# One inference step of a two-layer decoder: sample states, mixing blocks and the samples' last rows laid out anew

## The reference

```python
# layer 0, branch B: gated linear recurrence; for a sample one step from its stored state
inter = jnp.einsum('bthk,bhkv->bthv', qc * jnp.exp(cb), s)          # 8 samples, 4 heads, 128x128 states
...
# layer 1: causal mean pooling, four channel groups with trailing windows 2, 4, 8, 16
def pool_mixer(h, prev, pos0, w_groups, scale):
    ext = jnp.concatenate([prev, h], axis=1)                         # prev: the last 15 rows (zeros for the prompt)
    for gi, w in enumerate(POOL_WINDOWS):
        win_sum = csum[15 + 1 + t] - csum[15 + 1 + t - w]
        mixed = win_sum / min(w, pos + 1) - h[:, :, group gi]        # mean minus token
        outs.append(einsum('btc,cd->btd', mixed, w_groups[gi]))      # 256 x 256 per group
    return concatenate(outs, -1) * scale
# every layer
x = x + mix
x = x + hier_moe(rmsnorm(x), ...)    # top 1 of 4 groups, top 2 of its 8 SwiGLU experts, 32 experts in all
# at the end
y = rmsnorm(x, norm_final)           # for the prompt and for the samples
```

## Time and profile before

| what | us |
|---|---|
| median of 3 runs | 1458.81 (1457.67 to 1462.44) |
| profiled execution | 1456.91 |
| its span, first to last instruction | 1455.1 |
| PE busy in the span | 1254.0 (86%) |
| DVE busy | 357.2 (25%) |
| ACT busy | 256.1 (18%) |
| DMA, mean over the span | 339 GB/s |

### The profile page before, as it was taken

How to read it: one execution, slowest core, us unless ns; L and a number is a source line. 1 busy time by engine, 2 the same in 40 slices (tenths; PEclk the granted TensorE clock), 3 DMA queues, 4 the chain that set the end, 5 groups by cost and what they waited for, 6 DMA issues and landing times.

```text
span 1455.1 us, 14771 instructions
## 1 busy us (share of the span) xinstructions
PE 1254.0 (86%) x5968; PEld 614.9 (42%) x5968; DVE 357.2 (25%) x824; ACT 256.1 (18%) x440; POOL 83.7 (6%) x101
## 2 busy tenths in 40 slices
PE   7999999999999866878777798999978878888786
PEld 3688865544643322223222235863422222232222
DVE  2056477532431000010100007451010000010006
ACT  3243643333300000000000002520000000000002
POOL 1000000000000100000000000000000000000000
PEclk9999999999999999999999999899999998899998
DMA  9435657427489999999999999389999999999995
GB/s 347 107 71 183 219 162 220 115 88 318 172 349 428 425 401 422 428 427 425 426 427 427 425 413 367 142 305 420 427 428 426 426 430 426 426 427 425 427 415 209
DMA packets 82447, 492.95 MB, mean 339 GB/s; under 512 B 17197, under 2 KB 21965, under 8 KB 59350
## 3 DMA queue, kind: packets, MB, share of 16 engines
q1 hardware_dynamic: 65968, 449.35, 75.9%
q0 software_dynamic: 13568, 37.03, 7.6%
q10 hardware_dynamic: 2862, 5.91, 1.2%
HBM read 479.75 MB, written 36.56 MB: 355 GB/s over the span
## 4 chain that ended last, share of the span: by engine, by line
PE 50%; DMA 39%; DVE 7%; ACT 2%; issue 2%; SPq 0%; ACTq 0%; DVEq 0%
DMA ring<-in_moe_w 37%; PE ps L2241 21%; PE ps L1915 5%; PE ps L1908 4%; PE ps L2167 3%; PE ps L2279 2%; PE ps L2255 1%; PE ps L2226 1%; PE ps L2353 1%; PE ps L2307 1%; PE ps L2266 1%; DVE arena L1371 1%; PE ps L1957 1%; DMA arena<-i_rows 1%; PE ps L2296 1%
## 5 line engine op out<-in xcount | busy, mean ns | idle before, releaser
L2241 PE MATMUL ps<-ring,arena 128*64 128x512 f32 x1920 | 463.5, 640 | 118.5 <-DMA ring<-in_moe_w 117.4
L2241 PEld LDWEIGHTS ps<-ring,arena 128*64 128x64 f32 x1920 | 145.2, 147 | 432.4 <-issue 272.8
L1784 DVE TENSOR_TENSOR arena<-arena,ps 128x512 f32<-128x512 f32 x32 | 22.0, 688 | 775.3 <-ACT arena L1207 775.3
L2279 PE MATMUL ps<-ring,arena 128*64 128x512 f32 x832 | 186.0, 599 | 26.6 <-issue 14.1
L2279 PEld LDWEIGHTS ps<-ring,arena 128*64 128x64 f32 x832 | 68.8, 138 | 127.1 <-issue 112.7
L1207 ACT ACTIVATE arena<-ps 128x512 f32<-128x512 f32 x32 | 19.1, 597 | 584.1 <-PE ps L2241 584.1
L1908 PE MATMUL ps<-arena,ring 128*128 128x260 f32 x512 | 116.9, 387 | 0.9 <-ACT arena L942 0.9
L1908 PEld LDWEIGHTS ps<-arena,ring 128*128 128x128 f32 x512 | 97.0, 193 | 17.3 <-issue 1.7
L1215 ACT ACTIVATE arena<-ps,arena 128x1024 f32<-128x1024 f32 x32 | 35.6, 1114 | 321.2 <-PE ps L2279 276.5
L1915 PE MATMUL ps<-ring,arena 128*128 128x512 f32 x192 | 86.8, 599 | 0.0
L851 POOL DMA_INDIRECT arena<-hn_rows,arena x30 | 30.7, 1022 | 519.6 <-PE ps L2433 474.2
(11 more groups left out here) (312 smaller groups left out, 1053.9 us busy)
## 6 DMA issues: line engine op xcount, KB each, us to landing
ring<-in_moe_w SPq DMA_DIRECT2D x78, 4096.0 KB, 23.3
ring<-in_moe_w SPq DMA_DIRECT2D x40, 1024.0 KB, 12.5
arena<-in_moe_w SPq DMA_DIRECT2D x12, 2048.0 KB, 17.8
ring<-in_w_in SPq DMA_DIRECT2D x6, 2048.0 KB, 20.3
y_rows<-c_zero POOLq DMA_DIRECT2D x2, 4160.0 KB, 18.0
ring<-in_moe_w SPq DMA_DIRECT2D x4, 2048.0 KB, 20.3
ring<-y_rows SPq DMA_DIRECT2D x8, 1024.0 KB, 18.3
arena<-in_x_prompt SPq DMA_DIRECT2D x8, 512.0 KB, 6.2
```

The costliest lines, as they stand in the source:

```text
L2241: last = T.matmul(ps[r_, 2 + j, :], xgT[:, k, r_], w[:, k, :], start=(k == 0), stop=(k == KC - 1))
L2279: last = T.matmul(ps[r_, 5 + c, :], hactT[:, k, r_], w[:, k, c * 512:(c + 1) * 512], start=(k == 0), stop=(k == FC - 1))
```

## The change

**Sample states.** The masked queries become the weights: `qmask` holds for each head and sample 32 columns, of which one is the query and the others zero. The state is the moving operand (128 columns), the four heads write to the four groups of 32 partitions, and the 8 samples add up in PSUM. The result has a row per head and sample; DVE copies it, PE transposes it, and `sample_heads` comes one unit later, `sample_means` too.

**Mixing.** The matrix of the windows has 144 columns, 128 for the block and 16 for what the block carries into the next. One product per chunk does both. Eight chunks of 144 columns don't fit two banks of 512, so they come in three parts; the third reuses the first bank after ACT's copy. The copies lie in two buffers in turn. DVE adds the carry of the block before (`carry_added`), and the maps wait for it.

**Samples.** Their mixture is PE's 8 transposes of the normed rows, scaled and added to `mix_before` by DVE (`samples_mixed`). Maps and last rows put the four quarters of the channels in four column groups, and DVE adds them in four sums (`from_groups`).

**Tail.** PE adds the second row sets of tiles 0, 2 and 3 too, and for the samples both sets and x itself. The order is 0, 1, 2, NT, 3 on PE and SP; DVE's order is written out. The samples' normed rows come straight from PSUM: ACT squares, PE sums over the column groups with `fold`, ACT takes the root, DVE scales; four stores take them out. Five small loads for it are issued by POOL in layer 1's fourth pair.

```diff
@@ sample states, PE
-                        T.matmul(ps[:, 5, h * NB + b:h * NB + b + 1], stv[:, b, h, :], qf[:, h, b:b + 1], start=True, stop=True)
+                        T.matmul(ps[32 * h:32 * h + 32, 5, P:2 * P], qmask[:, h, 32 * b:32 * b + 32], stv[:, b, h, :],
+                                 start=(b == 0), stop=(b == NB - 1), skip_group_check=True, tile_position=(0, 32 * h))
...
+            def turn_sample_rows():                       # after project(SAMPLE0 + 2, 0)
+                pe.wait_ge(snorm_ready, 1)
+                T.transpose(ps[:, 5, 2 * P:3 * P], osr, ident).then_inc(s_read, 1)
@@ mixing, PE
             def mix(t):
-                n = rows_of(t)
                 pe.wait_ge(pooled_in, t + 1)
-                if t:
-                    pe.wait_ge(mixT_ready, 2 * t)
-                for k in range(KC):
...
-                        last = T.matmul(out, hall[:, t, cols], poolc[:, 0 if t == 0 else 1, g, :], start=True, stop=(t == 0))
-                        if t:
-                            last = T.matmul(out[:, 0:WINDOWS[-1]], hall[:, t - 1, cols], poolc[:, 2, g, 0:WINDOWS[-1]], start=False, stop=True)
...
+                pe.wait_ge(mixT_ready, 3 * t)
+                if t == NT:
+                    for k in range(KC):
+                        last = T.transpose(ps[:, 0, k * NB:(k + 1) * NB], hall[0:NB, NT, k * P:(k + 1) * P], ident[0:NB, 0:NB])
+                    last.then_inc(mix_done, 1)
+                    return
+                for part, (first, chunks, bank) in enumerate(MIX_PARTS):      # ((0, 3, 0), (3, 3, 1), (6, 2, 0))
+                    if part == 2:
+                        pe.wait_ge(mixT_ready, 3 * t + 1)
+                    for i in range(chunks):
+                        k = first + i
+                        last = T.matmul(ps[:, bank, i * (P + CARRY):(i + 1) * (P + CARRY)], hall[:, t, k * P:(k + 1) * P],
+                                        poolc[:, 0 if t == 0 else 1, k // 2, :], start=True, stop=True)
+                    last.then_inc(mix_done, 1)
 
             def maps(t):
                 if t:
                     pe.wait_ge(x_added, TILES + t)
+                    pe.wait_ge(mix_carried, t)
...
+                if t == NT:
+                    for k in range(2):
+                        for g in range(NG):
+                            last = T.matmul(ps[32 * g:32 * g + NB, 4, 0:256], mixT[NT % 2][:, 2 * g + k, 0:NB], poolw[:, g, k, :],
+                                            start=(k == 0), stop=(k == 1), skip_group_check=True, tile_position=(0, 32 * g))
@@ DVE between the layers
+                    def carry_added(t):
+                        dve.wait_ge(mixT_ready, 3 * t + 3)
+                        V.tensor_tensor(mixT[t % 2][:, :, 0:CARRY], mixT[t % 2][:, :, 0:CARRY], mixT[1 - t % 2][:, :, P:], ALU.add).then_inc(mix_carried, 1)
...
-                    for t in range(2):
-                        combine(0, t)
-                        add_last(0, t)
+                    combine(0, 0)
+                    combine(0, 1)
+                    add_last(0, 0)
+                    add_last(0, 1)
                     pooled_rows(0)
                     combine(0, 2)
                     add_last(0, 2)
...
                             add_mix(1, u - 1, u - 1)
+                        if u < NT:
+                            carry_added(u)
+                        if u == NT:
+                            samples_mixed()
                         if u == 1:
                             add_last(0, 3)
@@ the samples' sums, DVE
+            def from_groups(b):
+
+                for g in range(4):
+                    cols = slice(g * D // 4, (g + 1) * D // 4)
+                    last = V.tensor_tensor(x[0:NB, NT, cols], x[0:NB, NT, cols], ps[32 * g:32 * g + NB, b, 0:D // 4], ALU.add)
+                return last
@@ tail, DVE (before: per tile combine, add_last, normed rows of the tile before)
+            combine(1, 0)
+            combine(1, 1)
+            add_last(1, 0)
+            add_last(1, 1)
+            combine(1, 2)
+            combine(1, 3)
+            dve.wait_ge(router_in, 16 * 13)
+            final_rows(0)
+            add_last(1, 2)
+            final_rows(1)
+            final_rows(2)
+            add_last(1, 3)
+            sample_normed()
+            final_rows(3)
@@ tail, PE, in rows_of_last(t)
+                    if t == 3 and l == 1:
+                        pe.wait_ge(act_step, LAST_SQUARED)
+                        T.matmul(ps[:, LAST_BANK[NT] + 1, 0:1], fold, r_apart, start=True, stop=True).then_inc(sample_step, 1)
+                    if t == 0:
+                        pe.wait_ge(y_out, PAIRS * (l + 1))
+                        pe.wait_ge(memT_ready, 2 * l + 2)
@@ tail, ACT
+            def sample_root():
+
+                act.wait_ge(last_done, TILES + LAST_ORDER[1].index(NT) + 1)
+                nc.scalar.activation(junk_apart, ps[:, LAST_BANK[NT], 0:D // 4], ACT.Square, accum_out=r_apart).then_inc(act_step, 1)
+                act.wait_ge(sample_step, LAST_SUMMED)
+                nc.scalar.activation(r_apart, ps[:, LAST_BANK[NT] + 1, 0:1], ACT.Sqrt, bias=eps, scale=1.0 / D).then_inc(root[0], 1)
...
+                    t = LAST_ORDER[1][u]                  # (0, 1, 2, NT, 3)
+                    if t == NT:
+                        sample_root()
+                    else:
+                        act.wait_ge(moe_added, TILES + min(u, NT - 1) + 1)
+                        mean_root(4, t, x[:, t, :], spare)
```

More of the change, by code:

```diff
@@ L65 @@
 KEEP = 15
+CARRY = WINDOWS[-1]
 LEVELS = (128, 64, 32, 16)
@@ L322, in build @@
         ecmp = at(26900, NOV, NE)
+        fold = at(22216, P)
+        gain_apart = at(22216 + P, D // 4)
+        y_apart = at(22472 + P, D // 4)
+        junk_apart = at(22728 + P, D // 4)
+        r_apart = at(22984 + P, 1)
         fourth = [at(lo, PIECE) for lo in (0, 22216)]
@@ L734, in load_results @@
                 sp.wait_ge(y_stored, 16 * (PAIRS - 1) * (l + 1))
-                for t in range(TILES):
+                for t in LAST_ORDER[l]:
                     n = rows_of(t)
@@ L1154, in scaled_rows, with mixed_columns @@
                                          scale=rms[1][0:n, t:t + 1]).then_inc(hn_ready, 1)
-                def mixed_columns(t, half):
-                    act.wait_ge(mix_done, 2 * t + half + 1)
-                    if t and half == 0:
-                        act.wait_ge(pool_done, t)
-                    nc.scalar.activation(mixT[:, 4 * half:4 * half + 4, 0:rows_of(t)],
-                                         ps[:, half, :].rearrange("p (k c) -> p k c", k=4)[:, :, 0:rows_of(t)],
+                def mixed_columns(t, part):
+                    k, chunks, bank = MIX_PARTS[part]
+                    act.wait_ge(mix_done, 3 * t + part + 1)
+                    if t >= 2 and part == 0:
+                        act.wait_ge(pool_done, t - 1)
+                        act.wait_ge(mix_carried, t - 1)
+                    nc.scalar.activation(mixT[t % 2][:, k:k + chunks, :].rearrange("p k c -> p (k c)"), ps[:, bank, 0:chunks * (P + CARRY)],
                                          ACT.Copy).then_inc(mixT_ready, 1)
@@ L1185, in experts @@
                         if u < TILES:
-                            mixed_columns(u, 0)
-                            mixed_columns(u, 1)
+                            if u < NT:
+                                for part in range(3):
+                                    mixed_columns(u, part)
+                            else:
+                                act.wait_ge(pooled_in, TILES)
                             if u == NT - 1:
@@ L1514, in _ @@
                 m = u - STEP0
+                if u == SAMPLE0 + 2:
+                    sample_rows()
                 if 0 <= m < NSTEP:
@@ L2495, in rows_of_last @@
                         pe.wait_ge(x_in[t], 16 * l + 32)
+                        for c in range(2):
+                            for k in of_others:
+                                T.matmul(ps[0:n, LAST_BANK[t] + c, :], ident[0:n, 0:n], gat[t][0:n, k, c * 512:(c + 1) * 512],
+                                         start=(k == of_others[0]), stop=False)
+                    if t == 3 and l == 1:
+                        pe.wait_ge(act_step, LAST_SQUARED)
+                        T.matmul(ps[:, LAST_BANK[NT] + 1, 0:1], fold, r_apart, start=True, stop=True).then_inc(sample_step, 1)
@@ L2496, in rows_of_last @@
+                    if t == 0:
+                        pe.wait_ge(y_out, PAIRS * (l + 1))
+                        pe.wait_ge(memT_ready, 2 * l + 2)
                     for c in range(2):
-                        cols = slice(c * 512, (c + 1) * 512)
-                        for k in of_others:
-                            T.matmul(ps[0:n, LAST_BANK[t] + c, :], ident[0:n, 0:n], gat[t][0:n, k, cols], start=(k == of_others[0]), stop=False)
-                        last = T.matmul(ps[0:n, LAST_BANK[t] + c, :], memT[:, t * P:t * P + n], yst[:, cols],
```

(24 more changed lines are left out.)

140 lines of the change are left out of this document (80 added, 60 removed).

## The result

Median 1447.30 us (1443.53 to 1454.91, 9 executions) against 1459.76 (1457.66 to 1462.44, 9 executions) before: ratio 0.9929, 95% interval 0.9915 to 0.9944. The change takes 12.5 us off; 1446 (1438 to 1455) was predicted.

A forecast was written before the change was run, and what follows sets the result against it. The expert weight stream bounds both layers and halts between them; front, between-layer work and tail add to it. 1456.9 - 4.4 - 6.5 - 1.8 = 1444.2, plus 1.9 to the median: 1446 us, range 1438 to 1455.

The forecast's parts named there:

- A: Front, sample states: each of four parts falls from 1.81 to 0.68 us, -4.4 us in all.
- the first rival: Sample states: small weights load between the matmuls, not beside them; A is -2.7, time 1448 us; chance 0.08.
- B: Work between the layers, in seven steps including the clock: -6.5 us, between -10 and 0.
- Step 5: Between the layers, blocks 2 and 3: mixing 2.1 instead of 3.55 us, about 1.6 gained each, -3.3 us.
- Step 6: Between the layers, samples: PE takes 1.9 instead of 5.9 us, but DVE's routing and sum are late; -0.4 us.
- Step 4: Between the layers: block 1's gain lost behind DVE's carry and samples' sums; tile 0's router logits as before, zero gained.
- Step 7: Between the layers, clock: PE's time at 1.2 GHz loses 3.5 us where it lost 6.3, so -2.8 us.
- C: Tail after tile 1's rows land: fewer DVE additions in a new order, -1.8 us, between -3.2 and +1.
- Priced at nothing: Layer 1's five POOL loads (3 us if a gather came late), smaller constant load, samples' 64 KB load: no cost.
- B gives nothing: Between the layers: waits at the carry and copy repeat in blocks 2 and 3; 1452.5 us; chance 0.15.
- No slow clock: Between the layers: no time at the low clock, B = -10, time 1442.5 us; chance 0.10.
- The slower one: Between the layers: PE stays at 1.2 GHz from first router logits to first product, B = +19, 1471 us; chance 0.05.

The follow-up runs named there:

- changed_again: The changed kernel timed and profiled once more, with nothing altered: 1448.38 us, ratio 0.9927.
- no_a: The changed kernel with the old sample states (128x128 state as weights, one moving column): 1452.44 us, ratio 0.9958.
- no_c: The changed kernel with the old tail and the old last rows of the samples in both layers: 1448.79 us, ratio 0.9942.
- squares_early: The changed kernel with ACT squaring the samples' last rows ahead of tile 2's root instead of behind it: 1447.24 us, ratio 0.9915.
- loads_late: The changed kernel with POOL issuing the tail's five loads after the last results are stored: 1447.30 us, ratio 0.9922.
- wait_back: pe_samples plus two unread DVE additions of 8 rows where the samples' two additions had stood: 1447.37 us, ratio 0.9918.
- two: The changed kernel with the edits of pe_samples and squares_early together: 1442.12 us, ratio 0.9879.
- no_b: The changed kernel with the old work between the layers, the samples' last rows still in column groups: 1455.73 us, ratio 0.9978.
- pe_samples: The changed kernel with PE instead of DVE adding the samples' two gathered rows in layer 0 too: 1442.18 us, ratio 0.9885.
- mix_first: two, with block 2 mixed ahead of tile 0's router logits: 1438.45 us, ratio 0.9857.
- kept_busy: The changed kernel with 14 unread products of 384 columns where PE stood idle in layer 1's routing: 1445.88 us, ratio 0.9915.

## Why the prediction was right, and where it was not

**A, -4.4 predicted: -3.9 by the full-clock fronts, 4.2 +- 3.2 by the times.** The part is 0.57 instead of 0.68, and the column groups with 128 moving columns are not slower than those of the earlier trace rows: the first rival is out. The rows of i end at 179.02 instead of 183.13, -4.1. The Trainium skill (TensorE: Matmul & The Clock Gate, Part 3, "The mechanism") has loads beside matmuls only for different row groups. The trace disagrees: 16 loads into column groups, 16 products, 0.57 us in all, 0.036 a pair.

**B, -6.5 predicted: 79.4 to 73.8 in the two profiles; six profiles of the changed stage (after, changed_again, no_a, no_c, squares_early, loads_late) average 73.5, the two of the old one 79.8: -6.2. The sum was right, its split was not, so the agreement is in part luck: two misses of opposite sign.** (no_c has the old last rows of the samples; without it the average is 74.0.) Steps 5 and 6 rest on these lines of before, PE's timeline; those of after stand above.

```profile
926.99 0.47 PE L2205 MATMUL ps<-arena 128*128 128x128 f32 x2
...
935.21 1.97 PE L2307 MATMUL ps<-arena 128*128 128x36 f32 x16
...
946.66 1.95 PE L2307 MATMUL ps<-arena 128*128 128x36 f32 x16
...
953.26 3.82 PE L2353 MATMUL ps<-arena 128*128 128x128 f32 x32
```

- Step 1: block 0 starts 8.78 us after the last y instead of 10.05: -1.3 for -1.4. Step 2: maps of block 0 at 11.75 after it instead of 13.2 (11.6 forecast).
- Step 3: block 1 takes 3.20 (forecast 3.2 to 3.3), the carry 0.29 (0.3).
- Step 4, gain given back: DVE idle 1.33 (1.6), the samples' sums 1.70 (1.7), the turning waits, logits 25.89 after the last y instead of 26.30: -0.4 for 0. By wait_back and two the wait is worth 1.5 us by itself.
- Step 5: from block 3's mixing (920.58, before 926.99) to the router logits of tile 2, 6.95 instead of 8.22 at full clock in both: -1.3 a block for -1.6.
- Step 6, -0.4 forecast, was mis-sized in its parts: from the logits of tile 2 (927.53) to those of tile 3 (932.94) PE needs 5.4 us instead of 11.45 (935.21 to 946.66, with 3.4 at low clock), -6.0, but the rest to the first product grows from 17.0 to 22.1. PE waits 0.45, 1.10 and 1.58 us for DVE's sum and routing, as the step said, and then multiplies the columns of the first pair mostly at 1.2 GHz: 6.27 us at 943.02 against 3.82 before.
- **Step 7, the clock, -2.8 forecast, is the step that failed.** Low clock in the stage is 13.9 us in after and 13.6 before, the first stretch 3.4 us shorter and the second 3.4 longer; over the profiles it is 14.5 against 15.6, which at half rate is at most -0.5. Dense 144-column products did not hold it up, as they came after the logits at 907.12, where it had fallen, and ran mostly at 1.2 GHz themselves (3.94 us for block 2). The other steps gave 5.7 in place of 3.7 and made up for it.

**C, -1.8 predicted: about -1.0.** The times alone don't tell it from nothing (1.9 +- 4.0). The working is right from the landing of tile 1's rows on: 21.6 us to the end were forecast (1431.7 to 1453.3) and 21.55 measured, DVE's idle before tile 3's sum 1.63 for 1.4. What was mis-sized is the term ahead of it: the sum took over the landing 1.3 us after the last y; it came 2.7 us after it, and in the new tail DVE waits for it. The old tail doesn't feel that: in no_c the rows also landed 2.7 us after the last y, but DVE came to them only 4.4 us after it, as before. In the eight profiles with the new order and no earlier squares it is 21.5 to 21.9 us from the landing to the end, as forecast, and the landing comes 1.3 to 2.9 us after the last y; that is why their tails scatter.

**Priced at nothing.** Layer 1 took 469.3 instead of 466.7, 2.6 us more that the sum didn't have. Cut from y to y into its pairs of experts, the first took 29.1 us instead of 27.5, with a second stretch of low clock at 975: the seven profiles with two stretches in that pair took 28.6 to 29.2, the six with one 27.4 or 27.5. The fourth pair took 26.1 instead of 23.8, with a stretch at 1050.6; so did no_a and loads_late, which have one there (26.0 and 26.1), and the ten without took 23.8 to 24.2. Later pairs were shorter by 1.3 in sum. So low clock, which the prediction had between the layers alone, goes with the scatter of layer 1, too. The loads are acquitted: they start after the fourth pair, not in it, beside a fifth pair that took 31.4 us against 32.7 before, and loads_late gains nothing.

**Rivals.** "B gives nothing" and "the stream is not started earlier" are out by no_b and no_a. "No slow clock" does not describe this kernel, with 13.9 us of it; pe_samples and mix_first come nearer, with 3.4 and 6.8. The slower one stays out: low clock ended by itself after 6.8 us. For its sentence from the Trainium skill (the same page, Part 4) no run here sets a transpose against a matmul; the low stretch at 907.2 began 22 us ahead of the samples' transposes at 929.42, which so didn't bring it on. Tile 0's turning, eight transposes as well, does stand ahead of it (904.94), but it stands ahead of the logits in before, pe_samples and mix_first too, and there the clock stayed full through them. The second stretch is another matter: in changed_again it begins at 931.1, just behind the samples' transposes and in tile 3's turning, and in kept_busy and pe_samples likewise. What transposes do to the clock stays open.

## What to carry to other kernels

When an in-order engine gets a new wait, look at who needs the work queued behind it: here two additions of 8 rows (2.4 us) behind the carry held up TensorE, and moving them to that engine, at 1.07 us of its time, took 6.1 +- 4.5 us off, of which the wait explains 1.5 and the rest goes with the place of the low clock. Price a stage at full clock and give the clock its own term with both signs; here its places moved from execution to execution, and one profile of each kernel would have halved the gain. In a tail, ask whether the event that the new order hangs on keeps its place: the landing that the sum put 1.3 us after the last y came 1.3 to 2.9 us after it.

## What was not expected of the hardware

The granted clock fell to 1.2 GHz while PE was busy for 22.77 of 22.9 us (kept_busy), and it stayed full through a wait of 1.43 us and the 4.6 us after it (wait_back). In two executions of the same kernel it fell once in the same place (907) and then in others (941 in after, 931 and 945 in changed_again). Low stretches cost half of their length where PE is the path (logits 1.87 us at full, 3.57 at low) and next to nothing where DVE is (changed_again: 7.3 us more of it for 0.2).
